# Expert units of 128 rows in a 64-expert MoE: a whole unit for an expert of more than 32 rows, a quarter for one of up to 32

## The reference

```python
s = sigmoid(x @ w_router)                  # 384 x 64, float32
combine = weights of the 8 chosen experts, 0 elsewhere
hg = einsum('nd,edf->nef', x, w_gate)      # w_gate (64, 1024, 256)
hu = einsum('nd,edf->nef', x, w_up)        # w_up   (64, 1024, 256)
hid = silu(hg) * hu * combine[:, :, None]
y = einsum('nef,efd->nd', hid, w_down)     # w_down (64, 256, 1024)
```

## Time and profile before

| | |
|---|---|
| median of 3 runs | 1103.33 us (1097.87 to 1106.18) |
| the profiled execution | 1100.45 us |
| its span | 1098.6 us |
| TensorE busy | 1045.0 us, 95% |
| VectorE, ScalarE, GpSimd busy | 531.5, 357.0, 156.3 us |
| moved by DMA | 306.61 MB |
| first and last `gate_up` of the experts | 586.3 and 1042.8 us (start and end) |

### The profile page before, as it was taken

One profiled execution on the slowest core, in us unless ns is written; L12 is line 12 of the kernel. 1 busy time (PEld: TensorE's weight loads), 2 busy tenths in 40 slices (PEclk: granted clock), 3 DMA queues, 4 the chain that ended last, 5 costly groups with the idle time before them and its releaser, 6 DMA issues.

```text
span 1098.6 us, 14993 instructions
## 1 busy us (share of the span) xinstructions
PE 1045.0 (95%) x4876; PEld 700.3 (64%) x4876; DVE 531.5 (48%) x1110; ACT 357.0 (32%) x481; POOL 156.3 (14%) x136
## 2 busy tenths in 40 slices
PE   4999999999899999999998999999999999999975
PEld 2489888788788898884645455555545455454532
DVE  2233544354698965954633434433443324333357
ACT  3333444326444545501422222322222222222101
POOL 0020232000000000000010232322322313311000
PEclk9999999999999999999999999999999999999998
DMA  9999777355555332650287999999999999999592
GB/s 354 394 298 339 127 116 109 131 187 196 205 183 185 110 141 97 235 167 0 83 352 276 370 406 400 421 406 398 421 421 419 400 405 421 419 411 409 237 410 105
DMA packets 80896, 306.61 MB, mean 279 GB/s; under 512 B 12550, under 2 KB 16902, under 8 KB 65616
## 3 DMA queue, kind: packets, MB, share of 16 engines
q1 hardware_dynamic: 61264, 270.63, 62.4%
q0 software_dynamic: 12256, 26.80, 10.6%
q10 hardware_dynamic: 7328, 8.55, 2.2%
HBM read 285.31 MB, written 36.85 MB: 293 GB/s over the span
## 4 chain that ended last, share of the span: by engine, by line
PE 58%; DMA 2%; DVE 2%; ACT 1%; issue 1%; DVEq 0%; SPq 0%
PE PS L2066 16%; PE PS L2068 8%; PE PS L2091 4%; PE PS L1955 4%; PE PS L2052 3%; PE PS L1702 3%; PE PS L2081 2%; DMA bigA<-in_w_down 2%; PE PS L2082 2%; PE PS L2083 2%; PE PS L2023 2%; PE PS L2140 1%; PE PS L1945 1%; PE PS L1944 1%; PE PS L1943 1%; PE PS L2107 1%
## 5 line engine op out<-in xcount | busy, mean ns | idle before, releaser
L1102 POOL DMA_INDIRECT y_parts<-bigB,IDX x38 | 73.9, 1945 | 327.4 <-DVE bigB L1639 318.2
L2066 PE MATMUL PS<-bigB 128*128 128x512 f32 x224 | 101.7, 598 | 0.0
L1756 PE MATMUL PS<-bigB_r 128*128 128x384 f32 x288 | 98.6, 342 | 1.3 <-ACT bigB L788 1.3
L1758 PE MATMUL PS<-bigB_r,bigA_r 128*128 128x384 f32 x288 | 96.5, 335 | 0.0
L1757 PE MATMUL PS<-nT_r,bigB_r 128*128 128x384 f32 x288 | 96.3, 335 | 0.0
L1639 DVE TENSOR_SCALAR bigB<-PS,bigD 128x1024 f32<-128x1024 f32 x40 | 51.3, 1283 | 90.2 <-PE PS L2083 55.5
L2068 PE MATMUL PS<-bigA,bigB 128*64 128x512 f32 x208 | 94.8, 598 | 0.2 <-issue 0.2
L2069 PE MATMUL PS<-bigB 128*64 128x512 f32 x208 | 94.8, 599 | 0.0
L2066 PE MATMUL PS<-bigA,bigB 128*128 128x512 f32 x208 | 94.6, 598 | 0.0
L1247 DVE TENSOR_TENSOR bigA_r<-bigA,bigB_r 128x2048 fp32r<-128x2048 f32 x18 | 41.3, 2293 | 97.5 <-ACT bigB_r L814 97.5
L1605 DVE TENSOR_TENSOR bigB<-bigB,PS 128x256 f32<-128x256 f32 x40 | 16.8, 421 | 138.5 <-ACT bigB L998 138.5
(11 more groups left out here) (370 smaller groups left out, 2117.3 us busy)
## 6 DMA issues: line engine op xcount, KB each, us to landing
bigB<-in_w_gu SPq DMA_DIRECT2D x27, 2048.0 KB, 17.5
bigA<-in_w_gu SPq DMA_DIRECT2D x26, 2048.0 KB, 16.3
bigA<-in_w_in SPq DMA_DIRECT2D x17, 2048.0 KB, 11.2
bigB<-in_w_down SPq DMA_DIRECT2D x27, 1024.0 KB
bigA<-in_w_down SPq DMA_DIRECT2D x26, 1024.0 KB, 16.5
bigA<-in_w_ada SPq DMA_DIRECT2D x8, 2048.0 KB, 9.6
y_parts<-bigB SPq DMA_DIRECT2D x6, 2048.0 KB, 23.9
bigB<-in_w_ada SPq DMA_DIRECT2D x3, 2048.0 KB, 16.3
```

The source lines that it names most:

```text
L1102: pool.indirect_dma_start(y_parts, bass.IndirectOffsetOnAxis(ap=IDX[:, p, 1:2], axis=0), YS[:, p % 2, :], None, bounds_check=T * TOPK - 1, ...
L1756: mm(out, wh, nh, start=(k == 0), stop=False)
L1758: last = mm(out, wl, nh, start=False, stop=(k == KD - 1))
L2066: last = mm(PS[:, 2 + b, :], XT[:, b, k, :], GU_W[s][:, :, k, :], start=first, stop=stop)
```

## The change

An expert now gets whole units if it has more than 32 rows (`FEW`), and experts with up to 32 rows go four to a unit (a **quad** unit), each in 32 row slots. The pattern is six units long (`PERIOD`): five big, then one quad. Numbers of big experts fill the table of units from its start, those of small ones from its end. The weights of big units have two slots instead of four. A quad's weights come in six parts, each with a quarter of the gate and up weights (parts 0 to 3) or half of the down weights (4 and 5) of all four experts. Each part is four transfers of 512 KiB. Parts 4 and 5 go into the buffers of parts 0 and 1, once the first half of the quad's `gate_up` has read them. The quad's `gate_up` is eight times four products, each with 32 of the array's 128 columns, and it waits for the parts one by one. The host lays out an expert's gate and up weights with the eight k-slices outermost, so that a part is contiguous for each partition. At the end, the last four of the twelve transfers that bring `y_parts` back wait for the last `down`.

```diff
-HALF = P // 2
-BIG0 = NE
+FEW = P // 4
-UNITS_MAX = NE // 2 * 3
-BODY = 12
+PERIOD, BIGS = 6, 5
+UNITS_MAX = NE // 4 * PERIOD
+BODY = 2 * PERIOD
-WS, XGS, AHEAD, GAHEAD = 4, 3, 4, 3
+WS, XGS, AHEAD, GAHEAD = 2, 3, 4, 3
+def is_big(u):
+    return u % PERIOD < BIGS
+def big_number(u):
+    return u // PERIOD * BIGS + u % PERIOD
+def unit_of_big(b):
+    return b // BIGS * PERIOD + b % BIGS
...
-        WSLOT = [bigB[:, 0:6144], bigA[:, 6144:12288], bigA[:, 0:6144], bigB[:, 13824:19968]]
+        WSLOT = [bigB[:, 0:6144], bigA[:, 6144:12288]]
+        FOURTHS = [[bigA[:, i * D:(i + 1) * D] for i in range(4)],
+                   [bigB[:, 13824 + i * D:13824 + (i + 1) * D] for i in range(4)],
+                   [bigA[:, 4096:5120], bigA[:, 5120:6144], bigB[:, 17920:18944], bigB[:, 18944:19968]],
+                   [nT_flat[:, D:2 * D], nT_flat[:, 2 * D:3 * D], bigD[:, 0:D], bigD[:, D:2 * D]]]
...
+            def quad_part(experts, j):
+                for h, e in enumerate(experts):
+                    if j < 4:
+                        sp.dma_start(FOURTHS[j][h], matrix(w_gu, e)[:, j * D:(j + 1) * D]).then_inc(quad_loaded[j], 16)
+                    else:
+                        sp.dma_start(FOURTHS[j - 4][h], matrix(wd, e)[:, (j - 4) * D:(j - 3) * D]).then_inc(quad_loaded[j], 16)
...
             with sp.Fori(0, PASSES) as pas:
-                with sp.If(pas * BODY + 4 <= units):
+                with sp.If(pas * BODY + 3 <= units):
                     for p in range(BODY):
-                        i = pas * BODY + (1 + p)
-                        with sp.If(i + 4 <= units):
-                            sp.wait_ge(gu_ready, i + 1)
-                            for r, q in columns(pas * 8 + (p + 4) // 3 * 2, (p + 4) % 3):
-                                gate_up_of(r, q)
-                        with sp.If(i + 3 <= units):
-                            sp.wait_ge(dn_ready, i)
-                            for r, q in columns(pas * 8 + (p + 3) // 3 * 2, (p + 3) % 3):
-                                down_of(r, q)
+                        q = p + 1
+                        i = pas * BODY + q
+                        if is_big(q):
+                            b = big_number(q) + 2
+                            with sp.If(pas * BODY + (unit_of_big(b) + 1) <= units):
+                                sp.wait_ge(gu_ready, i + 1)
+                                big_gate_up(pas * BIGS_BODY + b, b % 2)
+                        if is_big(p):
+                            b = big_number(p) + 2
+                            with sp.If(pas * BODY + (unit_of_big(b) + 1) <= units):
+                                sp.wait_ge(dn_ready, i)
+                                big_down(pas * BIGS_BODY + b, b % 2)
+                        t = q // PERIOD
+                        first = lambda: pas * (-4 * QUADS_BODY) + (RTAB - 4 - 4 * t)
+                        if not is_big(q):
+                            with sp.If(pas * BODY + (t + 1) * PERIOD <= units):
+                                experts = quad_numbers(first())
+                                for j in range(2):
+                                    sp.wait_ge(quad_used, pas * (2 * QUADS_BODY) + (2 * t + j + 1))
+                                    quad_part(experts, 4 + j)
+                        elif q % PERIOD < 4:
+                            with sp.If(pas * BODY + (t + 1) * PERIOD <= units):
+                                if q % PERIOD == 0:
+                                    sp.wait_ge(gu_ready, i)
+                                    quad_part(quad_numbers(first()), 2)
+                                elif t > 0:
+                                    sp.wait_ge(dn_ready, i - 1)
+                                    quad_part(quad_numbers(first()), (3, 0, 1)[q % PERIOD - 1])
...
             for m in range(NT):
+                if m == NT - 1:
+                    sp.wait_ge(dn_ready, units)
                 for c in range(4):
...
             def gate_up(u, pas, p, ks):
...
+                    if k % 2 == 0:
+                        pe.wait_ge(quad_loaded[k // 2], pas * (64 * QUADS_BODY) + (quad_base[k // 2] + 64 * (n + 1)))
+                    for h in range(4):
+                        rows = slice(h * FEW, (h + 1) * FEW)
+                        last = mm(PS[rows, 2 + b, :], XT[:, b, k, rows], GU_Q[k // 2][h][:, k % 2, :], start=first, stop=stop)
+                    if k in (1, 3):
+                        last.then_inc(quad_used, 1)
```

More of the change, by code:

```diff
@@ L671, in _, with quad_numbers @@
+            def quad_numbers(first):
+                return [number(first + h) for h in range(4)]
+            def quad_part(experts, j):
[4 more added lines that the diff above has]
+                        sp.dma_start(FOURTHS[j - 4][h], matrix(wd, e)[:, (j - 4) * D:(j - 3) * D]).then_inc(quad_loaded[j], 16)
             sp.wait_ge(n2_out, 48)
-            sp.wait_ge(row_done, 1)
@@ L673, in _ @@
-            for r, q in ((BIG0, 0), (BIG0 + 1, 1), (1, 3)):
-                gate_up_of(r, q)
-                down_of(r, q)
             units = unit_count(sp)
-            sp.wait_ge(shd_ready, NT)
-            gate_up_of(0, 2)
-            down_of(0, 2)
-            with sp.If(units >= 4):
+            for b in range(2):
+                big_gate_up(b, b)
+                big_down(b, b)
+            with sp.If(units >= PERIOD):
+                quad_part(quad_numbers(RTAB - 4), 1)
+            sp.wait_ge(shd_ready, NT)
@@ L681, in _ @@
+            with sp.If(units >= PERIOD):
+                experts = quad_numbers(RTAB - 4)
+                quad_part(experts, 0)
+                quad_part(experts, 2)
+            with sp.If(units >= 3):
                 sp.wait_ge(gu_ready, 1)
-                gate_up_of(BIG0 + 2, 0)
+                big_gate_up(2, 0)
+            with sp.If(units >= PERIOD):
+                sp.wait_ge(sh_added, NT)
+                quad_part(quad_numbers(RTAB - 4), 3)
             with sp.Fori(0, PASSES) as pas:
-                with sp.If(pas * BODY + 4 <= units):
+                with sp.If(pas * BODY + 3 <= units):
@@ new lines, in _ @@
+                        t = q // PERIOD
[14 more added lines that the diff above has]
+                                    quad_part(quad_numbers(first()), (3, 0, 1)[q % PERIOD - 1])
+                                else:
+                                    with sp.If(pas >= 1):
+                                        sp.wait_ge(dn_ready, i - 1)
+                                        quad_part(quad_numbers(first()), (3, 0, 1)[q % PERIOD - 1])
@@ L1708, in index @@
                     pe.wait_ge(idx_done, u)
-                halves = 1 if s < 2 else 2
                 for m in range(NT):
-                    last = mm(PS[:, 4, 0:4 * halves], OH[:, b, m, :], RHS[:, b, 0:halves, m, :], start=(m == 0), stop=(m == NT - 1))
+                    last = mm(PS[:, 4, 0:4 * n], OH[:, b, m, :], RHS[:, b, 0:n, m, :], start=(m == 0), stop=(m == NT - 1))
                 last.then_inc(ix_ready, 1)
@@ L2082, in down @@
                             mm(out, HTL[:, b, k, :], DNH[:, k, cols], start=False, stop=False)
-                            last = mm(out, HTH[:, b, k, :], DNL[s][:, k, cols], start=False, stop=(k == 1))
+                            last = mm(out, HTH[:, b, k, :], DNL[n % 2][:, k, cols], start=False, stop=(k == 1))
                     last.then_inc(dn_ready, 1)
                     return
-                pe.wait_ge(dn_loaded[2], 16 * turn)
-                pe.wait_ge(dn_loaded[3], 16 * turn)
-                for hf in range(2):
-                    cols = slice(hf * 512, (hf + 1) * 512)
-                    for k in range(2):
-                        mm(PS[0:HALF, 6 + hf, :], HT[:, b, k, 0:HALF], DN_W[2][:, k, cols], start=(k == 0), stop=(k == 1))
-                        last = mm(PS[HALF:P, 6 + hf, :], HT[:, b, k, HALF:P], DN_W[3][:, k, cols], start=(k == 0), stop=(k == 1))
+                for k in range(2):
+                    pe.wait_ge(quad_loaded[4 + k], pas * (64 * QUADS_BODY) + 64 * (p // PERIOD + 1))
+                    for hf in range(2):
+                        for h in range(4):
+                            rows = slice(h * FEW, (h + 1) * FEW)
+                            last = mm(PS[rows, 6 + hf, :], HT[:, b, k, rows], DN_Q[k][h][:, hf * 512:(hf + 1) * 512],
+                                      start=(k == 0), stop=(k == 1))
                 last.then_inc(dn_ready, 1)
@@ L2098, in _ @@
             transposes(1, 1)
-            index(AHEAD, AHEAD % 3, AHEAD % 2)
-            gate_up(0, 1, 0, range(KD))
+            index(AHEAD, AHEAD)
+            gate_up(0, 0, 0, range(KD))
             units = unit_count(pe)
@@ L2117, in step @@
                     pe.wait_ge(hid_done, i)
-                    gate_up(i, turn, 1 + p, range(0, 4))
+                    gate_up(i, pas, 1 + p, range(0, 4))
                     hidden_t(i, p)
-                    index(i + AHEAD, (1 + p + AHEAD) % 3, (1 + p + AHEAD) % 2)
```

(3 more changed lines are left out.)

208 lines of the change are left out of this document (109 added, 99 removed).

## The result

The changed kernel takes **1221.62 us** (median of 4 runs, 1219.23 to 1225.92), the kernel before on the same chip 1104.58 us (median of 4, 1097.87 to 1106.18). The ratio is 1.1071 with an interval of [1.1031, 1.111]: 117 us slower. The forecast was 1146 us with a range of 1118 to 1170. The direction was right, the size was not. The profiled execution took 1225.92 us with a span of 1224.1.

What follows compares the result with a forecast made beforehand. The prediction took the kernel to be bound by TensorE with hardly any DMA to spare. TensorE's gain of 19.9 us and 63 us of waits gave +43 on 1100.45, and 2.9 more for the median: 1146 us, range 1118 to 1170.

Steps and rivals of the forecast that it cites:

- The bound: Experts' stretch before the change: TensorE bounds, DMA falls behind it, and 24.6 of about 27 us of lead are used.
- Rival A: Experts' loads: DMA had room, so waits vanish and the 19.9 us gain stays, 1083 us as median; chance 0.06.
- Units and bytes: Experts' loop: 39 units, 33 big and 6 quads, the sixth empty; four more expert loads, 12.6 MB; 32.2 MB a pattern.
- TensorE's part: Experts' units: TensorE needs 444.9 us instead of 464.8, gaining 19.9 if it never waits; 68.6 us a pattern.
- The quad's products: Quad's gate_up: 64 records in four column groups side by side take at most 7.4 us; a quad unit 12.5, like a pair.
- The places of the waits: TensorE waits in the first half of the quad's gate_up (part 1) and before its down (parts 4, 5).
- D: Rival: the change doesn't do what it says, e.g. the empty quad is skipped; about 11.6 us less, 1134; chance 0.03.
- The step that failed: DMA queue in each full pattern: idles 1.8 us, so a pattern costs 80.1 us, 11.6 over TensorE's own.
- 385 GB/s for short runs: Quads' loads in 4 KiB runs: at this rate 12.7 us more; taken as 0, with 12.7 kept as an end.
- Rival C: After TensorE's waits: slower clock, shorter runs and idle queue add 25 to 45 us, 1170 to 1190; chance 0.11.
- B: Rival for DMA: rate reaches 435 GB/s or queue gaps fill; waits of about 25 us, 1105 to 1112; chance 0.05.
- Small edits: Table of units, index lists, issue of parts and last y_parts transfers: each hidden beside other work, 0 us.

Runs made afterwards that it cites:

- b2: The kernel before, with TensorE leaving out 8 of the 12 products of a big unit's down (less exact results): 1097.81 us.
- b1: The kernel before, with each weight load of the loop issued one unit later: 1116.2 us.
- a8: The changed kernel, with all quad parts issued in the loop moving 64 bytes a partition instead of 4 KiB (wrong results): 1089.61 us.
- a1: The changed kernel, with SyncE issuing a quad's parts 4 and 5 ahead of the big unit's down load: 1165.2 us.
- a5: The changed kernel, with the empty sixth quad's parts loaded 64 bytes wide a partition instead of 4 KiB: 1198.23 us.
- a2: The changed kernel, with a quad's part 3 issued right behind part 2, and parts 0 and 1 one unit earlier each: 1187.17 us.
- b3: The kernel before, with each gate and up load split into four 512 KiB transfers in 4 KiB runs, each down load into two: 1120.23 us.
- a3: The changed kernel with both reorderings of SyncE's issues: parts 4 and 5 ahead of the down load, and parts 0, 1 and 3 earlier: 1156.97 us.
- a4: The changed kernel, with TensorE doing 12 needless products before the wait for part 1 and 7 before that for part 4: 1225.43 us.
- a6: The changed kernel with both reorderings of SyncE's issues and the empty quad's parts 64 bytes wide a partition: 1147.68 us.

## Why the prediction was right in direction and wrong in size

**Right.** *The bound.* The kernel before lives on a shrinking reserve of DMA: 50 us less of TensorE brought 7 (b2), one unit less of lead cost 11 (b1). Rival A, that DMA had room, is refuted. *Units and bytes.* 39 units, 33 of them big (528 records of `gate_up`, 16 each), 318.86 MB, 32.0 MB a pattern. *TensorE's part.* 69.5 us a pattern against 68.6. The gain was 14.4 us (a8; its interval is 7 to 18) against 19.9; of the missing 5.5 us, 1.8 are the table of units, which lay on TensorE's path and not at 0: from its first product to the next one of the shared expert it is 562.26 - 558.23 = 4.03 us in a1, 556.13 - 553.92 = 2.21 before. The rest was not taken apart; the 0.9 us a pattern is of its size. *The quad's products.* The whole `gate_up` of the first quad, 645.49 to 653.30, takes 7.81 us, as the pair's 7.83. *The places of the waits*, and that the empty quad runs and pays: D, that it is skipped, is refuted by a5. In a5 it is worth 23.4 us, twice the 11.6 of the forecast, since the empty quad pays the full price of a pattern, 25.8.

**The step that failed** is, in the prediction's words, "It idles between 0 and 5 us; I take 1.8, nearer the low end, because a queue that is behind idles least", and with it "One pattern costs 80.1 us, 11.6 over TensorE's own." Measured are 94.4 us, 25.8 over 68.6. In the terms of the prediction:

- Idle DMA is 0.14 x 94.4 = 13.2 us a pattern, not 1.8. This is 11.4 us a pattern. The silence of SyncE was put at 12 to 17 us and is 24.6; and there is a second one of 19.3 us that the prediction doesn't have. It had said that the silence grows "with the quad's wait for its part 1", and then allowed that wait at most 5 us, where it is 10.8 to 12.4. The waits hang together: the late part 1 holds back the `down` behind it, that `down` holds back parts 4 and 5, the wait for these holds back the loads of the next pattern. The first link is shown by a2: with part 1 in time the same silence is 16.0 us (812.75 to 828.79 us there). The last is read from the order of the program alone: in a1 parts 4 and 5 come in time, and TensorE waits for part 1 as long as before. A queue that is behind does not idle least if its next entry waits for an engine that waits for the queue.
- The rate while busy is 394 GB/s, not 411: 32.2 MB take 81.7 us, not 78.3, 3.4 a pattern. The prediction had 385 GB/s for short runs as an end and took 0; b3 shows 398 on average for such runs, between the two ends, and a3 395 with this kernel's own loads. Why the rate is lower is open.

Both together are 14.8 us, and 80.1 + 14.8 = 94.9 against 94.4. Five quads pay it: four patterns at 25.8, and the last, whose own waits are 12.14 + 5.37 + 1.89 us and whose slow products take 3.42 and 3.22 us where 1.90 and 1.92 are their time, some 22. The first pattern (645.49 to 725.17) lies 11.1 over 68.6, where 5 was predicted. That makes 4 x 25.8 + 22 + 11.1 = 136 us of waits and lost time against 63, less the 14.4: +122, where the profiled span shows 1224.1 - 1098.6 = +125.5.

That the order, and not the bytes or the units, makes the larger part is shown by a1 to a3: nothing but the order of SyncE's instructions changed, and 65 of the 117 us went. With both orders the kernel takes 1157 us, the pattern 82.0: close to the 1146 and 80.1 of the forecast, which had priced a queue that hardly empties. The rest of a3, 53 us over before, is what the change costs in this order, in which DMA has next to no pause left (whether another layout of buffers would do better was not tried): nine experts' bytes for six units of which TensorE needs 69 us.

**Rival C**, "waits cost clock and order as well", was the nearest. Its mechanisms are all there, and its price of 1170 to 1190 was too low for the same reason: "up to 3 us more of idle queue a pattern". Its clock part of 1.8 us for each long wait is what the rows show (3.64 against 1.90), but a4 shows that 2.9 us a pattern come back when it is removed. B, the partial case, needed a higher rate; the rate fell.

**Small edits.** The index lists show in no wait. The `y_parts` transfers were said to be hidden, since the first eight would start some 12 us before the last `down` is done. They are issued from 1175.14 us, less than 4 us before that (1178.9), and TensorE waits for such a transfer:

```profile
1180.92 5.39 PE L2213 MATMUL PS<-bigA,K 128*128 128x512 f32 x8 [2.00 <-DMA bigA<-y_parts]
```

It cost little: from the end of the last `down` to the end of the span it is 45.2 us, and 43.6 before, where the same product waited 1.65 us. In the profiled execution the experts' first transposes begin at 588.04 us, before at 582.79; 1.8 of that are the table. The clock of the stretch from 540 to 580 us was 0.91 to 0.92 there and 1.00 in a1, so the other 3 belong to this execution.

## What to carry to other kernels

When two engines are both near full, a change has to be priced by when each load is issued and when it is needed, not by bytes over a period. Walk the issuing engine's program in order and write beside each load the event that its wait names: every load behind it inherits that event, though its own buffer has long been free. Where a load waits for an engine that in turn waits for loads, the delay comes back in every round, and the first thing to try is to issue what is free ahead of what must wait; it cost nothing here and gave back 56 us. As the pauses of DMA go, order has less to give: the second reordering brought 34 us alone and 8 on top of the first, and what helped after that was fewer bytes (a6).

## What the runs showed of the hardware that was not expected

- After waits of 5 to 12 us TensorE's granted clock fell (0.84 in the stretch of the wait, 0.64 in the next), and the first sixteen records took 3.64 us instead of 1.90, at 1.2 in place of 2.4 GHz; the next stretch was back at 1.00. Busy filling kept the clock but moved the total time little.
- The time that SyncE takes to issue transfers varies: four of 512 KiB took 1.88 to 3.08 us in the changed kernel and 4.84 us in b3, against 0.34 for a single one. A full share alone doesn't lengthen it: at 907.62 us four took 1.92 us with DMA at a share of 1.03. What does was not tried; in the changed kernel the long ones are those of part 5, issued right behind part 4's four.
- The Trainium skill (DMA: Bandwidth & Descriptors, Bandwidth) advises transfers of 1 MiB or more. For a queue that is kept full, halving and quartering the transfers cost 3% of the rate and 15 us of 1104 (b3), not the nothing that the prediction had taken.
- The fit that the prediction took from the same page of the Trainium skill (section Anatomy of one DMA — SWDGE (gpsimd) path) has 2.0 us for each transfer, and is given there for transfers that GpSimd issues. By it the 212 transfers that b3 has more would cost 424 us one after another, an estimate. The trace of b3 doesn't agree with that for loads that SyncE queues behind each other: it was 15 us.
